# A hybrid decoder layer on one core: matmuls on ones ahead of the first tokens, another order of the first loads and rows, slot codes 1000 apart, two one-hots by ScalarE, half waits in a pair

## What is computed

```python
h = rmsnorm(x, ln1_g)
u, va, q, k, v = split(h @ w_in)            # five groups of 512 columns; q and k get rope
a_out = u * (causal_w @ rmsnorm(va) + b_s)  # per 128-row chunk, 8 groups
b_out = merge(dilated_attn(q, k, v) for (window, dilation) in ((128,1),(512,4),(2048,16)))
x = x + concat(a_out, b_out) @ w_out        # sample rows attend to cached keys and values
h = rmsnorm(x, ln2_g)
g = argmax(softmax(h @ w_rg + b_rg))        # one group of 4
gates = top-2 of 8 experts inside the group
x = x + sum(gate_e * (silu(h @ w_gate[e]) * (h @ w_up[e])) @ w_down[e])
y = rmsnorm(x, lnf_g)                       # also returned: rotated k, v, normalised va
```

## Time and profile before

| what | us |
|---|---|
| median of 3 runs | 414.27 (412.69 to 415.22) |
| the profiled execution, its own time | 414.16 |
| its span on the core | 412.2 |
| TensorE busy | 379.6 |
| VectorE busy | 214.1 |
| ScalarE busy | 153.2 |
| GpSimd busy | 71.2 |

### The profile page before, as it was taken

How to read it: one execution, slowest core, us unless ns; L and a number is a source line. 1 busy time by engine, 2 the same in 40 slices (tenths; PEclk the granted TensorE clock), 3 DMA queues, 4 the chain that set the end, 5 groups by cost and what they waited for, 6 DMA issues and landing times.

```text
span 412.2 us, 6452 instructions
## 1 busy us (share of the span) xinstructions
PE 379.6 (92%) x2478; PEld 204.3 (50%) x2478; DVE 214.1 (52%) x440; ACT 153.2 (37%) x330; POOL 71.2 (17%) x59
## 2 busy tenths in 40 slices
PE   1999999998989999998989999879999999999694
PEld 1445544443434434454533466765556555563381
DVE  2979799998464574365351535732222312221194
ACT  4735211335444474455332455212222312222053
POOL 0003646441000100000000001231323233211000
PEclk9999999999999999999999999999999999999898
DMA  8992978853223244730159998999999999995395
GB/s 280 362 302 83 352 222 254 268 206 101 105 86 120 105 153 121 263 129 1 38 218 411 408 415 298 384 343 406 405 408 411 411 408 406 405 404 211 126 361 204
DMA packets 42466, 109.16 MB, mean 265 GB/s; under 512 B 7880, under 2 KB 8648, under 8 KB 42432
## 3 DMA queue, kind: packets, MB, share of 16 engines
q1 hardware_dynamic: 36000, 94.71, 62.4%
q0 software_dynamic: 5856, 12.81, 8.2%
q10 hardware_dynamic: 576, 1.19, 0.9%
HBM read 100.00 MB, written 16.94 MB: 284 GB/s over the span
## 4 chain that ended last, share of the span: by engine, by line
PE 61%; DVE 17%; DMA 11%; ACT 3%; issue 3%; POOL 2%; SPq 1%; DVEq 0%; POOLq 0%; ACTq 0%
PE bank L1668 20%; PE bank L2025 10%; DVE weights_split L1114 5%; PE bank L2044 5%; DMA big<-tokens_between 4%; DMA tokens_split<-h_rows,middle 4%; DVE sT L1161 3%; PE bank L1763 3%; PE bank L2014 3%; PE bank L1777 3%; PE bank L1642 3%; PE bank L1755 3%; PE bank L1971 2%; POOL big L680 2%; PE bank L1903 2%
## 5 line engine op out<-in xcount | busy, mean ns | idle before, releaser
L1668 PE MATMUL bank<-weights_split,tokens_split 128*128 128x512 f16 x576 | 133.4, 383 | 2.6 <-DVE x L1372 1.4
L1668 PEld LDWEIGHTS bank<-weights_split,tokens_split 128*128 128x128 f16 x576 | 54.9, 99 | 73.5 <-issue 11.4
L680 POOL TENSOR_TENSOR big<-big,middle 128x1536 f32<-128x1536 f32 x8 | 28.6, 3569 | 57.1 <-DMA middle<-sample_q 38.5
L2025 PE MATMUL bank<-big,tokens_split 128*64 128x256 f32 x320 | 36.7, 382 | 1.5 <-ACT tokens_split L1015 1.5
L1555 DVE TENSOR_TENSOR middle<-bank,middle 128x128 f32<-128x128 f32 x16 | 4.7, 292 | 53.8 <-ACT middle L1020 53.8
L2025 PEld LDWEIGHTS bank<-big,tokens_split 128*64 128x64 f32 x320 | 22.9, 137 | 12.6 <-ACT tokens_split L1015 2.0
L727 POOL DMA_INDIRECT expert_rows<-weights_split,middle x16 | 16.1, 1005 | 65.7 <-PE bank L2014 42.1
L1114 DVE SCALAR_TENSOR_TENSOR weights_split<-middle,weights_split 128x1024 f16<-128x1024 f32 x16 | 25.7, 1639 | 0.4 <-ACT weights_split L784 0.3
L891 ACT ACTIVATE middle<-bank 128x128 f32<-128x128 f32 (+3 forms) x32 | 13.9, 435 | 30.0 <-PE bank L1763 29.7
L696 POOL DMA_DIRECT2D h_rows<-middle x5 | 2.7, 543 | 117.9 <-ACT middle L982 117.9
L1020 ACT ACTIVATE middle<-bank 128x128 f32<-128x128 f32 x16 | 4.4, 278 | 48.7 <-PE bank L2025 48.7
(11 more groups left out here) (211 smaller groups left out, 564.2 us busy)
## 6 DMA issues: line engine op xcount, KB each, us to landing
big<-in_w_gate SPq DMA_DIRECT2D x10, 1024.0 KB, 12.3
big<-in_w_up SPq DMA_DIRECT2D x10, 1024.0 KB, 16.2
big<-in_w_down SPq DMA_DIRECT2D x10, 1024.0 KB, 18.0
middle<-in_w_in SPq DMA_DIRECT2D x16, 512.0 KB, 6.2
big<-in_cache_win_k SPq DMA_DIRECT2D x24, 256.0 KB, 4.3
middle<-in_cache_win_v SPq DMA_DIRECT2D x24, 256.0 KB, 4.4
big<-in_w_out SPq DMA_DIRECT2D x8, 512.0 KB, 8.0
big<-expert_rows SPq DMA_DIRECT2D x8, 512.0 KB, 7.1
```

Of the source, the lines that this page charges most:

```text
L680: nc.gpsimd.tensor_tensor(prod[:, :, :], kring[:, b % 2], qb[:, b % 2, :].unsqueeze(1).to_broadcast([P, NPAT, W]), ALU.mult).then_inc(prod ...
L1668: ins = T.matmul(out, (hT if rows is None else rows)[:, high_low, k if rows is None else k - 4, tokens], wg[:, place, part, k, columns], s ...
L2025: ins = T.matmul((ptb, ovb)[b][e * CAP:(e + 1) * CAP, 0:2 * FE], xT[:, b, k, e * CAP:(e + 1) * CAP], places[slot][:, 0:2, e, k * FE:(k + 1 ...
```

## The change

1. Start: the gain is loaded by SP behind x0, x1 behind the first weight piece, `small` behind the rope tables. Both leave ScalarE's queue, which keeps the identity.
2. TensorE waits for the identity only before its first transposes, and runs 52 more matmuls on ones before them. `turn_h` of tile 1 comes inside the q projection of tile 0 (behind row block 1), that of the sample tile inside the projection of tile 1 (behind row block 3). A projection waits for the halves of its tile one by one. ScalarE and VectorE get another order: the first weight piece and tile 0 first, then tile 1, then the other pieces.
3. Slot codes are 1,000 times the place in the pair plus the rank, and the iota jumps to 1,000 at column 64. The operation that marked ranks of 64 or more and the one that added it fall away; the iota takes a second operation, once, in the attention stage.
4. One-hots 0 to 7 are compared by VectorE, 8 and 9 made by ScalarE as Relu(1 - Abs(code - iota)), two dependent operations each.
5. ScalarE's copy of a pair's rows waits for four of the eight transposes; `gate_up` waits for ScalarE's half at the start and for VectorE's half before row block 4.
6. Behind the weights, the reads of the rows count on the semaphores `x_in` (up to 32) and no longer on `x_back`.

```diff
@@ SP
             sp.dma_start(x[:, 0, :], xp[0]).then_inc(x_in[0], 16)
-            sp.dma_start(x[:, 1, :], xp[1]).then_inc(x_in[1], 16)
+            sp.dma_start(gain[:, :], ln1_g.partition_broadcast(P)).then_inc(gain_in, 16)
...
                 for i, dst in enumerate(pieces(n)):
                     sp.dma_start(dst, src[:, 2 * i:2 * i + 2, :]).then_inc(w_loaded[n // 4][i], 16)
+                    if n == 0 and i == 0:
+                        sp.dma_start(x[:, 1, :], xp[1]).then_inc(x_in[1], 16)
...
             sp.dma_start(sin[:, :, :], const[:, C_ROPE + NT * HD:C_LTRI].rearrange("p (t n) -> p t n", t=NT)).then_inc(rope_in, 16)
+            sp.dma_start(small[:, :], const[:, C_M100:C_END]).then_inc(small_in, 16)
@@ ScalarE
-            act.dma_start(gain[:, :], ln1_g.partition_broadcast(P)).then_inc(gain_in, 16)
             act.dma_start(ident[:, :], const[:, C_IDENT:C_IDENT + P]).then_inc(ident_in, 16)
-            act.dma_start(small[:, :], const[:, C_M100:C_END]).then_inc(small_in, 16)
...
             square(ENTRY[0])
-            square(ENTRY[1])
             split_high(0, 0)
             turn_h(ENTRY[0])
+            square(ENTRY[1])
             for i in range(1, PIECES):
                 split_high(0, i)
+            turn_h(ENTRY[1])
             square(ENTRY[2])
-            turn_h(ENTRY[1])
...
+            act.wait_ge(slots_ready, 1)
+            for i, kt in enumerate(range(BY_COMPARE, 2 * NT)):
+                hot = onehot_p[:, kt, :]
+                nc.scalar.activation(hot, iota_h, ACT.Abs, scale=-1.0, bias=r1[:, kt:kt + 1]).then_inc(onehots_a, 1)
+                act.wait_ge(onehots_a, 2 * i + 1)
+                nc.scalar.activation(hot, hot, ACT.Relu, scale=-1.0, bias=1.0).then_inc(onehots_a, 1)
...
-                act.wait_ge(turned, n + 1)
+                act.wait_ge(half_turned, n + 1)
@@ VectorE
             norm(ENTRY[0])
+            split_low(0, 0)
+            low_h(ENTRY[0])
             norm(ENTRY[1])
-            low_h(ENTRY[0])
-            for i in range(PIECES):
+            for i in range(1, PIECES):
                 split_low(0, i)
...
-                    V.tensor_copy(iota_h, iota[:, 0:P])
+                    V.tensor_copy(iota_h[:, 0:CAP], iota[:, 0:CAP])
+                    V.tensor_scalar(iota_h[:, CAP:P], iota[:, CAP:P], float(ODD - CAP), None, ALU.add)
...
-            V.tensor_scalar(r2, rk, float(CAP), 1000.0, ALU.is_ge, ALU.mult)
-            step(V.scalar_tensor_tensor(out=r1, in0=par, scalar=float(CAP), in1=rk, op0=ALU.mult, op1=ALU.add))
-            step(V.tensor_tensor(r1, r1, r2, ALU.add))
+            V.scalar_tensor_tensor(out=r1, in0=par, scalar=float(ODD), in1=rk, op0=ALU.mult,
+                                   op1=ALU.add).then_inc(slots_ready, 1)
+            dve.wait_ge(slots_ready, 1)
...
-                for kt in range(2 * NT):
+                for kt in range(BY_COMPARE):
@@ TensorE
-            pe.wait_ge(ident_in, 16)
+            def warm_up(count):
+
+                for i in range(count):
+                    T.matmul(sbk[1][:, 0:P], ones[:, :], ones[:, :], start=True, stop=True)
+
             def turn_h(t):
+                if t == ENTRY[0]:
+                    pe.wait_ge(ident_in, 16)
...
-                wait_turned_out(pe, ("h", 2 * t + 1))
                 free_wait(pe, UNIT[unit])
                 for k in range(KD):
+                    if k % 4 == 0:
+                        wait_turned_out(pe, ("h", 2 * t + k // 4))
...
                     part_of(unit, k)
+                    if unit == ("q", ENTRY[0]) and k == 1:
+                        turn_h(ENTRY[1])
+                    elif unit == ("q", ENTRY[1]) and k == 3:
+                        turn_h(ENTRY[2])
...
+            warm_up(52)
             turn_h(ENTRY[0])
-            turn_h(ENTRY[1])
             project(("q", 0))
-            turn_h(ENTRY[2])
             project(("q", 1))
...
-                    pe.wait_ge(onehots, kt + 1 if part == 0 else 2 * NT + 1)
+                    if part == 0 and kt >= BY_COMPARE:
+                        pe.wait_ge(onehots_a, 2 * (kt - BY_COMPARE + 1))
+                    else:
+                        pe.wait_ge(onehots, kt + 1 if part == 0 else BY_COMPARE + 1)
...
+                    if k == 3:
+                        ins.then_inc(half_turned, 1)
...
                 pe.wait_ge(xt_a, n + 1)
-                pe.wait_ge(xt_d, n + 1)
...
                 for k in range(KD):
+                    if k == 4:
+                        pe.wait_ge(xt_d, n + 1)
```

More of the change, by code:

```diff
@@ L168 @@
 BY_PE, BY_VECTOR = (1, 3), (0, 2)
+BY_COMPARE, ODD = 8, 1000
 TASKS = [(i, h) for i in range(4) for h in range(HEADS)]
@@ L417, in build @@
         zeroed = sem("zeroed")
+        half_turned, slots_ready, onehots_a = sem("half_turned"), sem("slots_ready"), sem("onehots_by_scalar")
         second_in = [sem(f"second_rows_in{i}") for i in range(2)]
@@ L430, in build @@
         mixed, sq3, y_ready = sem("mixed"), sem("sq3"), sem("y_ready")
-        x_stored, x_back, gain_back = sem("x_stored"), [sem(f"x_back{t}") for t in range(NT)], sem("gain_back")
+        x_stored, gain_back = sem("x_stored"), sem("gain_back")
         xp = x_prompt.rearrange("a (t p) d -> (a t) p d", p=P)
@@ L645, in _ @@
             for t in READ_ORDER:
-                sp.dma_start(x_end[0:rows_of(t), t, :], dram_rows(x2_dram, t)).then_inc(x_back[t], 16)
+                sp.dma_start(x_end[0:rows_of(t), t, :], dram_rows(x2_dram, t)).then_inc(x_in[t], 16)
             sp.dma_start(gain_end, lnf_g.partition_broadcast(P)).then_inc(gain_back, 16)
@@ L1513, in more_tables @@
                 step(V.tensor_scalar(hi, xi, 6, None, ALU.logical_shift_right), dv_more)
-                V.scalar_tensor_tensor(out=slot_no, in0=par, scalar=float(CAP), in1=lo, op0=ALU.mult, op1=ALU.add)
+                V.scalar_tensor_tensor(out=slot_no, in0=par, scalar=float(ODD), in1=lo, op0=ALU.mult, op1=ALU.add)
                 step(V.scalar_tensor_tensor(out=r4, in0=hi, scalar=float(PAIRS), in1=pair_no, op0=ALU.mult, op1=ALU.add), dv_more)
@@ L1590, in add_rows @@
                 xt = x_end[0:n, t, :]
-                dve.wait_ge(x_back[t], 16)
+                dve.wait_ge(x_in[t], 32)
                 dve.wait_ge(rows_in[t], 32)
@@ L2077, in _ @@
             for i, t in enumerate(BY_PE):
-                pe.wait_ge(x_back[t], 16)
+                pe.wait_ge(x_in[t], 32)
                 for half in range(2):
```

## The result

The changed kernel takes 411.69 us (median of 17 executions, 410.38 to 414.06), the kernel before on the same chip 414.27 (also 17; one of them took 1,689.37 us, which moves the median by 0.02). The ratio is 0.9932, with a 95% interval of 0.991 to 0.9955: about 2.6 us, under 1%. The profiled execution took 411.46, its span is 409.5 and not 412.2. So 2.7 us of span have to be found.

The account below looks back on a forecast made before the run. TensorE held 61% of the chain; at the start VectorE was almost gapless and TensorE slow at the lower clock. Start 2.2, routing 0.6 and half waits 0 made 2.8: 414.16 to 411.4 us, range 409.4 to 414.2.

Parts of the forecast that it names:

- Loads: Start: with the new order of loads the first weight piece lands at 8.05 us instead of 9.55.
- Step (f): End of the start: after the last rotations the sample's q is stored at 30.65 us, not 32.86; gain 2.2.
- The ones: Start: 52 more warm-up matmuls buy TensorE's higher clock level from the first q matmul on, 0.22 us each in tile 0.
- The prediction's own sign of being wrong: Start: the forecast would be wrong if matmuls of tile 0 took 0.43 us instead of 0.22.
- level falls back: Rival, chance 0.17: TensorE's clock falls again before the q matmuls; the start gives only 0.5 to 0.7, time 413.0 us.
- the front: The start of the kernel up to the store of the sample's q, forecast to gain 2.2 us.
- Routing: Simpler slot codes save 0.28, eight instead of ten VectorE one-hots 0.34; the table comes 0.6 us earlier.
- Half waits: Pairs 0 and 1: earlier copies and gate/up gain 0 because gathers follow; bound 0.7; rival that they count, chance 0.12.
- Table loads: Rival, chance 0.05: ScalarE's Abs and Relu for one-hots each need a function load of 1.28 us; time 416.4 us.
- Stream: Rival, chance 0.1: expert weights use up their 1.05 us slack, the gain of 0.6 is lost at the last pair; 412.0.
- Sum: Whole kernel: gains of 2.2, 0.6 and 0 make 2.8, taken from 414.16 to give 411.4 us; chance 0.5.

Follow-up runs that it names:

- no half waits: The changed kernel, but a pair's copies and gate/up wait for all eight transposes as before; 412.6 us, ratio 0.997.
- the traces with filler: Kernels with 42 instead of 30 filler matmuls before the first gather; medians 411.06 and 411.38 us with half waits, 411.3 without.
- weights 5 held back: The changed kernel, but SP issues pair 5's up and down weights only after the first pair's rows are transposed; 413.01 us, ratio 0.9956.
- The start alone: The kernel before with only parts 1, 2 and 6 of the change, routing and half waits as before; 412.86 us, ratio 0.9974.
- more filler: The changed kernel with 42 instead of 30 filler matmuls before the first gather; 411.06 us, ratio 0.9888.

## Why the prediction held, point by point

- **Loads.** Forecast 8.05 for the first piece, measured 8.09. VectorE's half of it ends at 10.44 (10.3), the low halves at 11.63 (11.6), the norm at 13.02 (13.4), the further pieces at 16.43 (16.85), and the rotation of tile 1 starts at 25.01 (25.0). Following one engine in the order of its own instructions gave each point within 0.4 us.
- **Step (f), the store.** Forecast 30.65, measured 30.98, a gain of 1.88 for 2.2. I took SP to be free at 30.4, "because the queue is full". VectorE ended at 30.78, 0.13 late; SP was free at 30.94, 0.54 late, because `gcol` and `rbias` keep it for 3.41 and 3.37 us. The run with those loads on GpSimd's queue shows it. But the prediction also took the store for the link that carries the gain, and no more than 2.4 for usable because of the queue. Both are wrong: in ten of fourteen traces the second product keeps to VectorE's rotation, and *no half waits*, with its store 1.98 earlier than before, starts it 2.60 earlier (41.40 for 44.00). What the start gave the changed kernel is 2.07 at the second product and 1.97 at the ranks, so the 0.2 us by which the queue held the store cost nothing.
- **The ones.** The prediction counted the higher level "from the first q matmul on". That is half wrong: the first six of tile 0 ran at the lower level in four of the ten traces with the ones (the changed kernel's two among them) and at the higher one in six. The prediction's own sign of being wrong, tile 0 at 0.43 a matmul, thus came true for six of its 24. The two groups differ in what came before: the 52 ones took 4.02 to 4.18 us in the four, and 2.26 to 2.43 us without work followed; they took 4.52 to 5.24 in the six, and 1.21 to 1.95 followed. The number of ones is fixed, so the earlier the level rises, the sooner they run out. Ones up to the first transposes were not tried. The rival *level falls back* came true in its mechanism, not in its price: it put the front at 0.5 to 0.7, and the front gave 1.88. It took the level to stay low through tile 0; it stayed so for 3 us, under VectorE's split. The rotation of tile 1 was forecast at 25.0 with the level high and came at 25.01 with it low; the six traces with it high have 24.41 to 24.50. That this point was met to the hundredth is luck: a pace put 0.5 us too slow made up for the fall. By VectorE's last rotation the ones are worth 0.3 us in one run without them (31.05 for 30.78) and 1.5 in the other (32.29); against the traces with the level high (30.17 to 30.26) about 0.8 and 2.1. Little of that difference arrives: in four of those six the first rank matmul comes at 262.71 to 263.09, where the first run without ones has it at 262.73.
- **Routing.** Forecast 0.6, measured 0.45. The 0.28 of the slot code is right (ranks to the first one-hot 2.56 before, 2.28 after), the eight one-hots too (1.71 to 1.39). Mis-sized was ScalarE's operation: I took 0.28 from a copy; Abs took 0.40 and 0.39, Relu 0.31, so the pair took 1.38 us and not 1.24. So ScalarE ends with VectorE and not before it, and TensorE's last one-hot ends 0.40 behind ScalarE's last where it ended 0.25 behind VectorE's: that is 0.15.
- **Half waits.** Forecast 0. From table to pair 2 the traces with filler are 0.2 to 0.35 us longer with half waits, and the medians are level (411.3 and 411.38), though their intervals are wider than that. The waits at the second and the fourth gather were forecast at 0.9 and 1.1 and are 0.88 and 1.31.
- **Table loads.** None stands before the four operations. The Trainium skill ("ScalarE: Activation LUTs", on table sets) has relu and abs in every set; the trace agrees.
- **Stream.** TensorE doesn't wait for weights in the changed kernel. Weights 5 are issued 2.42 us earlier (268.76 for 271.18), as the table is, so the stream won what the routing won, and the slack stayed. That the slack is real, and about that small, the run with weights 5 held back shows.
- **Sum.** 1.97 to the ranks and 0.45 behind them are 2.42; the other 0.28 of the 2.7 lies behind the table, where 0.46 was lost by pair 2 and 0.74 won again, 0.45 of it at the wait for the rows of the last stage. No term of the sum has that. So the forecast of 411.4 is met by 411.69 with a sound account of the start and the routing, two terms too large (by 0.2 and 0.15), and some luck on the other side. The chances were given for 410.0 to 418.4, the range for 409.4 to 414.2; the result lies in both.

**What stays open.** The start alone measured 0.26%, 1.05 us, where its store came 2.0 us earlier. In its trace 1.1 us went with the late q, held by the queue and by a read of 4.64 us; what makes that read take 3.1 or 4.7 us was not found. Besides, the kernel before has its level high at tile 0 in some executions; how often was not counted. The fall behind the first gather is a chance of each execution; it stood behind waits of 2.06, 2.25 and 2.94 us in three traces and not behind 1.35 to 1.64 in seven others (the kernel before among them), but what makes a first gather take 3.8 or 6.0 us was not found. None of the versions beats the changed kernel beyond its interval.

## What to carry to other kernels

Follow the engine that is busy nine tenths of a stretch, instruction by instruction in the new order; up to 17 us each point came within about 0.4 us. Then ask what the next stage starts on, in more than one trace: the chain of one execution ran through a queue that two small loads of 3.4 us each had held up, and yet the next stage kept to VectorE within 0.03 us in ten traces of fourteen. A warm-up with a fixed number of matmuls ends sooner the sooner it works; leave no gap behind it that you have not measured. Where two waits stand in a row, on a copy and on a transfer released earlier, shortening the first one only lengthens the second.

## What the runs showed of the hardware

- A load of 4-byte pieces (`gcol`) and one of a row broadcast to 128 partitions (`rbias`) keep SP's queue for 3.0 to 3.5 and 3.2 to 4.9 us. From GpSimd they cost 1.09 and 0.62 us of issue.
- GpSimd's product of 128x1536 in f32 takes 3.44 us. Started 0.3 to 1.2 us before VectorE's split of weights ended, it took 3.64 to 4.47 and ended 3.3 us behind the split, in ten traces.
- Behind 52 ones that took 4.02 to 4.18 us and 2.26 to 2.43 us without work the level fell ahead of the first q matmuls; behind 4.52 to 5.24 and 1.21 to 1.95 it did not (four traces and six).
- The first gather takes 3.8 to 6.0 us; the second and fourth of the changed kernel, with megabytes of weights issued around them, 8.41 and 7.57.
- At 128x128 in f16 ScalarE's Abs with a bias per partition takes 0.40 us, Relu 0.31, where VectorE's compare takes 0.17.
- The level of TensorE's clock at the eight matmuls that open the last stage differs from run to run (3.67 or 5.37 us). It moves the end by less: the last stage takes 27.5 to 27.9 us at the lower level, 25.8 to 27.1 at the higher, since its last matmuls can then wait for expert rows, as the timeline of the kernel with more filler shows:

```profile
382.28 3.67 PE L2107 MATMUL bank<-big,ident 128*128 128x512 f32 x8 [2.60 <-issue]
...
396.51 7.10 PE L2115 MATMUL bank<-big,middle 128*128 128x512 f32 x16 [0.73 <-DMA big<-expert_rows]
```
